# Threshold search on VectorE alone, rotations spread over four slabs

## The chip, the cores and the metric

The kernel runs on one core of one Trainium2 chip. The metric is the device time of one execution in microseconds (us), as a median of several runs. The core's engines are called as in the profile: PE (TensorE matmul) with PEld (its weight load), DVE (VectorE), ACT (ScalarE), POOL (GpSimd) and SP (SyncE, which here only issues DMAs). Each engine works through its own list of instructions in order; semaphores tie the lists together.

## What is computed

The program is two whole transformer blocks over 1024 tokens of width 1024. Only the second block's input projection and the selection of keys matter here:

```python
h = rms_norm(x, norm_mix[i])
proj = h @ w_in[i]
(r_q, r_k, r_v, r_g, d_q, d_c, d_pe, d_g,
 i_q, i_k, i_w) = jnp.split(proj, split_at, axis=-1)
r_q = rotary(r_q.reshape(B, S, RET_HEADS, RET_DK), positions, RET_THETA)
r_k = rotary(r_k.reshape(B, S, RET_HEADS, RET_DK), positions, RET_THETA)
...
q_pe = rotary(d_q[..., :DSA_ROPE], positions, ROPE_THETA)
...
score = jnp.einsum('bth,bths->bts', wi, rel).astype(jnp.float32)
score = jnp.where(valid[None], score, -jnp.inf)
top_val, top_idx = lax.top_k(score, n_sel)     # n_sel = 256
```

The kernel does not sort. For each query row it finds the value of the 256th largest score by fixing the 32 bits of a float one after the other: for each bit it counts how many scores lie at or above a candidate, and keeps the bit if there are at least 256.

## The kernel before

`build` runs ten stages one after the other; at the end of a stage's block all engines meet. The stage of this case is `stage_project`.

**TensorE** computes the projection in `product` (L1538 to L1542): a float32 product is three matmuls of 128x512 (high by high, high by low, low by high), here called a triple. The weights come in pieces of 128x512, one for each of eight k's of a slab of 512 columns. Slabs `R_Q` and `R_K` are made in four halves of four token tiles (`queries`); the score matmuls stand between those triples. `R_V`, `R_G`, `D_Q` and `D_G` follow in a loop over `slab(j)`, with all eight token tiles for each piece, so a piece of them is eight triples. A bank is filled again only when it has been evacuated (`ev`).

**A piece's way**: SP loads it (L2049) into one of four buffers, once PE has finished the piece four before it (`um`). ACT copies it to the rounded high part (`split`, L2142), POOL subtracts to get the low part (L2249), and PE waits for that (`lo`). So a piece can be ready three pieces ahead of PE.

**ACT** also evacuates the banks to `PJ` (`evacuate`, L2147), with Silu for the two gates. During the search its list is written by a planner: `begins` and `ends` foretell with `TRIPLE` = 0.68 us when PE will want a piece and when a bank is ready, `BIT` = 4.9 us is a bit of the search, and `slab_work` puts splits and evacuations between the bits accordingly.

**POOL** also rotates `R_Q` and `R_K`. A `turn` of one token tile is one `cmul` of six tensor_tensors (L374 to L379). In the passes n = 5 and 6 (the slabs `R_V` and `R_G`) one turn follows every piece's subtraction, sixteen in all. In the last pass four smaller ones rotate `D_Q`.

**DVE** makes the scores `NM` (L2295) and then searches. The score rows of the six token tiles with more than 256 keys have 384, 512, 640, 768, 896 and 1024 elements. In `count` DVE compares the two widest to 0 or 1 (L2305, uint8 into `junk`) and ACT sums them (L2228, `counted`); the four narrower ones DVE compares and sums in one instruction (L2308). Three instructions on 128x6 integers then follow: the comparison with 256 (L2311, after the wait for ACT), the keeping of the bit (`copy_predicated`, L2318), and the next candidate (L2316). After the stage comes `stage_retention`, whose first matmuls are at L2360.

Of the kernel before, what the change touches and what calls it, by code (L numbers as in the profile page):

```python
# [17 lines left out]
F32 = mybir.dt.float32  # L18
# [10 lines left out]
KT = D // P  # L29
# [1947 lines left out]
def stage_project(K):  # L1977
# [33 lines left out]
    cnt, need = columns(NB), columns(NB)  # L2011
    K.thr, K.cnt, K.need = thr, cnt, need
    w_in = [K.sem(f"pj_win{s}") for s in range(NR)]
    names = "prm hi lo um tm ev angr tab rope rms itr iev smm relr used cmp counted chain pchain".split()
    S = {n: K.sem("pj_" + n) for n in names}
    R_Q, R_K, R_V, R_G, D_Q, D_G = range(6)
    slabs = [None, R_Q, R_K, R_V, R_G, D_Q, D_G]
# [7 lines left out]
    for half in range(2):  # L2025
        quota[turned[half]] = (half + 1) * KT * NH
    ahead = [KT + q // NH + 2 for q in quota]
    TRIPLE, BIT = 0.68, 4.9

    def begins(u):  # L2030
        return TRIPLE * ((u - KT) * NH if u < 5 * KT else 4 * KT * NH + (u - 5 * KT) * NT) - TRIPLE * beside

    def ends(q):
        j, i = 2 + q // NT, q % NT
        return begins((3 + i // NH + 1) * KT if j == 2 else (j + 3) * KT) - TRIPLE * (NH - i % NH if j == 2 else NT - i)

    def table(t, lo, n, heads):
        return t[:, :, lo:lo + n].unsqueeze(2).to_broadcast([P, NT, heads, n])

    with nc.Block() as block:  # L2040
# [92 lines left out]
        @block.scalar  # L2133
        def _(act):
            arrived = [0] * NR

            def split(j, ks):
                cols = N_MIX if j == 0 else HALF
                for k in ks:
                    arrived[k % NR] += 32 if j == 0 else 16  # L2140
                    act.wait_ge(w_in[k % NR], arrived[k % NR])
                    nc.scalar.activation(part[k % NR][0][:, 0:cols], raw[k % NR][:, 0:cols], ACT.Copy).then_inc(S["hi"], 1)  # L2142

            def evacuate(j, i, bank):
                dst = K.MS[:, i, :] if j == 0 else K.PJ[:, slabs[j], i, :]
                func = ACT.Silu if slabs[j] in (R_G, D_G) else ACT.Copy
                nc.scalar.activation(dst, bank[:, 0:N_MIX if j == 0 else HALF], func).then_inc(S["ev"], 1)  # L2147

            def take_half(half):
                for i in range(NH):  # L2150
                    if i < NH - 1:
                        act.wait_ge(S["tm"], NT - 1 + half * (NH - 1) + i + 1)
                    else:
                        act.wait_ge(S["um"], (half + 2) * KT)
                    evacuate(1 + half // 2, half % 2 * NH + i, K.bank[i + (NH if half == 3 else 0)])

            def take_first():
                for i in range(NT):
                    if i < NT - 1:
                        act.wait_ge(S["tm"], i + 1)  # L2160
                    else:
                        act.wait_ge(S["um"], KT)
                    evacuate(0, i, K.bank[i])

            def take_one(q):
                j, i = 2 + q // NT, q % NT
                if j == 2:
                    half = 2 + i // NH
                    if i % NH < NH - 1:
                        act.wait_ge(S["tm"], NT - 1 + half * (NH - 1) + i % NH + 1)  # L2170
                    else:
                        act.wait_ge(S["um"], (half + 2) * KT)
                elif j == len(slabs) - 1:
                    act.wait_ge(S["um"], NP * KT)
                elif i < NT - 1:
                    act.wait_ge(S["tm"], NT - 1 + 4 * (NH - 1) + (j - 3) * (NT - 1) + i + 1)
                else:
                    act.wait_ge(S["um"], (j + 3) * KT)
                evacuate(j, i, K.bank[i])

            def slab_work(made, taken, until):
                while True:
                    more = made < NP * KT and begins(made) - 8.0 < until
                    done = taken < NT * (len(slabs) - 2) and ends(taken) - 1.5 < until
                    if not more and not done:
                        return made, taken
                    if more and (not done or begins(made) - 8.0 < ends(taken) - 1.5):
                        split(made // KT, range(made % KT, made % KT + 1))
                        made += 1
                    else:  # L2190
                        take_one(taken)
                        taken += 1

            split(0, range(4))
            act.wait_ge(S["angr"], 1)
            nc.scalar.activation(sin[:], red[:], ACT.Sin).then_inc(S["tab"], 1)
            nc.scalar.activation(cos[:], quar[:], ACT.Sin).then_inc(S["tab"], 1)
            split(0, range(4, KT))
            split(1, range(3))
            take_first()  # L2200
            split(1, range(3, lead // NH + 1))
            for i in range(NT):
                act.wait_ge(S["itr"], i + 1)
                b = K.bank[4 + i % 4]
                nc.scalar.activation(iqT[:, :, i * P:(i + 1) * P], b[:, 0:2 * P].rearrange("p (m t) -> p m t", m=2), ACT.Copy)
                nc.scalar.activation(ikT[:, i * P:(i + 1) * P], b[:, 2 * P:3 * P], ACT.Copy).then_inc(S["iev"], 1)
            act.wait_ge(S["rms"], 1)
            nc.scalar.activation(ss[:], ss[:], ACT.Sqrt).then_inc(S["rms"], 1)
            made = KT + lead // NH + 1
            for n in range(len(groups)):  # L2210
                for m in range(4 * n, 4 * n + 4):
                    i, h, c, e = pieces[m]
                    act.wait_ge(S["smm"], n + 1)
                    if m >= 4:
                        act.wait_ge(S["used"], m - 3)
                    nc.scalar.activation(rel[m % 4][:, 0:e - c], K.bank[4 + m % 4][:, 0:e - c], ACT.Relu, scale=IDIM ** -0.5).then_inc(S["relr"], 1)
                while made < ahead[n]:
                    split(made // KT, range(made % KT, made % KT + 1))
                    made += 1
                if n in turned:  # L2220
                    take_half(turned.index(n))
            act.wait_ge(S["used"], len(pieces))
            made, taken = slab_work(made, 0, 3.0)
            for b in range(32):
                for j in range(NB - 2, NB):
                    x = junk[:, packed(j + 2)]
                    act.wait_ge(S["cmp"], 2 * b + j - (NB - 2) + 1)
                    nc.scalar.activation(x, x, ACT.Copy, accum_out=cnt[:, j:j + 1]).then_inc(S["counted"], 1)  # L2228
                made, taken = slab_work(made, taken, 3.0 + BIT * (b + 1))
            slab_work(made, taken, 1.0e6)  # L2230

        @block.gpsimd
        def _(pool):
# [11 lines left out]
            for n in range(NP):  # L2245
                cols = N_MIX if n == 0 else HALF
                for k in range(KT):
                    pool.wait_ge(S["hi"], n * KT + k + 1)
                    g.tensor_tensor(part[k % NR][1][:, 0:cols], raw[k % NR][:, 0:cols], part[k % NR][0][:, 0:cols].bitcast(F32), ALU.subtract).then_inc(S["lo"], 1)  # L2249
                    if k == 0 and n == 1:  # L2250
                        pool.wait_ge(S["tab"], 2)
                    if n in (5, 6):
                        turn(n - 4, 0, FREQ_R, slice(k, k + 1))
                    elif n == NP - 1 and k >= 4:
                        turn(5, FREQ_R, FREQ_A, slice(2 * (k - 4), 2 * (k - 3)))

        @block.vector
        def _(dve):
# [41 lines left out]
            for i in range(NT):  # L2300
                link(v.memset(K.NM[0:RCHUNK, packed(i)][:, P * (i + 1) - RCHUNK:], LOW))

            def count(bound, b):
                for j in range(NB - 2, NB):
                    v.tensor_scalar(junk[:, packed(j + 2)], K.NM[:, packed(j + 2)], bound(j), None, ALU.is_ge).then_inc(S["cmp"], 1)  # L2305
                for j in range(NB - 2):
                    x = K.NM[:, packed(j + 2)]
                    last = v.tensor_scalar(junk[:, packed(j + 2)], x, bound(j), 0.0, ALU.is_ge, ALU.add, accum_out=cnt[:, j:j + 1])  # L2308
                link(last)
                dve.wait_ge(S["counted"], 2 * (b + 1))  # L2310
                link(v.tensor_scalar(keep[:], cnt[:], TOPK - 0.5, None, ALU.is_ge))  # L2311

            count(lambda j: 0.0, 0)
            link(v.tensor_scalar(thr[:], keep[:], 1, None, ALU.subtract))
            for bit in range(30, -1, -1):
                link(v.tensor_scalar(cand[:], thr[:], 1 << bit, None, ALU.bitwise_xor))  # L2316
                count(lambda j: cand[:, j:j + 1].bitcast(F32), 31 - bit)
                link(v.copy_predicated(thr[:], keep[:], cand[:]))  # L2318


def stage_retention(K):
# [708 lines left out]
```

## Time and profile before

| what | value |
|---|---|
| median of 3 runs | 2340.78 us (2338.63 to 2342.23) |
| the profiled execution, its own time | 2344.68 us |
| its span | 2342.9 us |
| PE busy | 2152.0 us, 92% |
| DVE busy | 1261.3 us, 54% |
| ACT busy | 783.0 us, 33% |
| POOL busy | 414.2 us, 18% |
| mean granted TensorE clock | 0.958 |

Times in the rows count from the span's start. A number in square brackets at the end of a row of the timeline is the engine's idle time just before the row, with what ended it. "PEclk" is the clock granted to TensorE as a share of the full 2.4 GHz. The stage in question ends at about 1856 us, and the search begins at 1613 us.

### The profile page before, as it was taken

Reading aid. Unit: us, or ns where it says so; the run is one execution under the profiler, and the core shown is the slowest. Engines: PE = TensorE matmul, PEld = TensorE weight load, DVE = VectorE, ACT = ScalarE, POOL = GpSimd, SP = SyncE. Lnnn points to the kernel's source line nnn. Section 1 sums busy time; section 2 is a strip of 40 time slices with the busy share of each in tenths; the row PEclk is TensorE's granted clock in tenths of the full one; section 3 lists DMA queues with packets and bytes.
Section 4 is the critical chain, followed back from the end, with each engine's and each line's share of the span. In section 5 each row is a group of like instructions: output and inputs, shape, how many; then the busy total and the mean of one; then the engine's idle time right before and its main releaser. Section 6 shows DMA issues by size and latency. Waiting matters only on the chain. (4 is left out here: it accounts for less than half of the span.)

```text
span 2342.9 us, 27640 instructions
## 1 busy us (share of the span) xinstructions
PE 2152.0 (92%) x10421; PEld 1578.9 (67%) x10421; DVE 1261.3 (54%) x2170; ACT 783.0 (33%) x1396; POOL 414.2 (18%) x485
## 2 busy tenths in 40 slices
PE   7998999996979999999999995989789877989998
PEld 3744564593448888888888884956567774758876
DVE  6581893395753333224553225289999077862433
ACT  2222111210013322223443224266446244761415
POOL 2900011040000000000000002224782450300110
PEclk9999999997979999999999997999999998989999
DMA  8533110003223332343343332212111102003201
GB/s 316 153 128 121 39 36 1 1 1 135 72 81 96 93 98 85 94 153 108 111 123 109 89 90 67 60 46 77 32 41 39 33 1 80 1 1 126 72 1 72
DMA packets 187510, 180.55 MB, mean 77 GB/s; under 512 B 12982, under 2 KB 157686, under 8 KB 184074
## 3 DMA queue, kind: packets, MB, share of 16 engines
q1 hardware_dynamic: 184426, 168.61, 23.1%
q0 software_dynamic: 2880, 10.49, 1.2%
q8 instruction: 67, 1.10, 0.2%
q14 instruction: 41, 0.34, 0.0%
q10 hardware_dynamic: 96, 0.02, 0.0%
HBM read 165.18 MB, written 12.60 MB: 76 GB/s over the span
## 5 line engine op out<-in xcount | busy, mean ns | idle before, releaser
L1729 DVE TENSOR_TENSOR ff_part<-ff_raw,ff_part 128x1024 fp32r<-128x1024 f32 (+2 forms) x152 | 164.9, 1085 | 434.7 <-ACT ff_part L1643 434.6
L1643 ACT ACTIVATE ff_part<-ff_raw 128x1024 fp32r<-128x1024 f32 (+2 forms) x152 | 144.0, 948 | 433.8 <-PE ps L1542 431.6
L1540 PE MATMUL ps<-h,ff_part 128*128 128x512 f32 x704 | 275.6, 391 | 4.4 <-DVE ff_part L1729 4.4
L1541 PE MATMUL ps<-h,ff_part 128*128 128x512 f32 x704 | 274.9, 390 | 0.0
L1542 PE MATMUL ps<-h,ff_part 128*128 128x512 f32 x704 | 274.9, 390 | 0.0
L1540 PE MATMUL ps<-pj_part,h 128*128 128x512 f32 (+1 forms) x448 | 182.2, 407 | 39.1 <-POOL pj_part L2249 28.1
L1541 PE MATMUL ps<-pj_part,h 128*128 128x512 f32 (+1 forms) x448 | 176.6, 394 | 0.0
L1542 PE MATMUL ps<-pj_part,h 128*128 128x512 f32 (+1 forms) x448 | 176.0, 393 | 0.0
L1540 PEld LDWEIGHTS ps<-h,ff_part 128*128 128x128 f32 x704 | 132.8, 189 | 32.2 <-DVE ff_part L1729 4.8
L1542 PEld LDWEIGHTS ps<-h,ff_part 128*128 128x128 f32 x704 | 132.7, 189 | 27.8
L1541 PEld LDWEIGHTS ps<-h,ff_part 128*128 128x128 f32 x704 | 132.9, 189 | 27.6
L1540 PEld LDWEIGHTS ps<-pj_part,h 128*128 128x128 f32 x448 | 86.4, 193 | 77.5 <-POOL pj_part L2249 34.7
L1540 PE MATMUL ps<-ff_hid,ff_part 128*128 128x512 f32 x352 | 136.9, 389 | 0.0
L1541 PE MATMUL ps<-ff_hid,ff_part 128*128 128x512 f32 x352 | 136.9, 389 | 0.0
L1542 PE MATMUL ps<-ff_hid,ff_part 128*128 128x512 f32 x352 | 136.9, 389 | 0.0
L2249 POOL TENSOR_TENSOR pj_part<-pj_raw,pj_part 128x512 fp32r<-128x512 f32 (+1 forms) x72 | 93.8, 1308 | 195.3 <-ACT pj_part L2142 195.2
L1540 PE MATMUL ps<-w_end,se_hT 128*128 128x512 f32 x256 | 106.9, 418 | 0.4 <-DVE se_hT L2959 0.4
L1000 PE MATMUL ps<-mx_w,HT 128*128 128x272 f32 (+1 forms) x320 | 106.2, 493 | 0.0
L1542 PE MATMUL ps<-w_end,se_hT 128*128 128x512 f32 x256 | 99.9, 390 | 0.0
L1541 PE MATMUL ps<-w_end,se_hT 128*128 128x512 f32 x256 | 99.7, 389 | 0.0
L1542 PEld LDWEIGHTS ps<-pj_part,h 128*128 128x128 f32 x448 | 86.5, 193 | 17.0
L2228 ACT ACTIVATE pj_junk<-pj_junk 128x896 uint8<-128x896 uint8 x64 | 64.0, 1002 | 98.6 <-DVE pj_junk L2305 96.9
(572 smaller groups left out, 4005.0 us busy)
## 6 DMA issues: line engine op xcount, KB each, us to landing
ff_raw<-in_w_ffn_in SPq DMA_DIRECT2D x88, 512.0 KB, 3.7
s_wm<-in_w_mod SPq DMA_DIRECT2D x16, 1024.0 KB, 4.9
pj_raw<-in_w_in SPq DMA_DIRECT2D x64, 256.0 KB, 2.6
ff_raw<-in_w_ffn_out SPq DMA_DIRECT2D x32, 384.0 KB, 3.3
ff_raw<-in_w_ffn_out SPq DMA_DIRECT2D x32, 320.0 KB, 3.1
mod_w<-in_w_mod SPq DMA_DIRECT2D x8, 1024.0 KB, 9.0
mod_x<-in_x SPq DMA_DIRECT2D x8, 512.0 KB, 14.5
w_out<-in_w_out SPq DMA_DIRECT2D x4, 1024.0 KB, 8.6
```

Of the source, the lines that this page charges most:

```text
L1000: mm = nc.tensor.matmul(bank[:, 0:cols], lhs, rhs, start=(k == 0), stop=(k == KT - 1))
L1540: nc.tensor.matmul(out, w[0], x[0], start=first, stop=False)
L1541: nc.tensor.matmul(out, w[0], x[1], start=False, stop=False)
L1542: return nc.tensor.matmul(out, w[1], x[0], start=False, stop=last)
L1643: nc.scalar.activation(part[s % 2][0][:, 0:n, :], raw[s][:, 0:n, :], ACT.Copy).then_inc(hi, 1)
L1729: v.tensor_tensor(part[s % 2][1][:, 0:n, :], raw[s][:, 0:n, :], part[s % 2][0][:, 0:n, :].bitcast(F32), ALU.subtract).then_inc(lo, 1)
L2228: nc.scalar.activation(x, x, ACT.Copy, accum_out=cnt[:, j:j + 1]).then_inc(S["counted"], 1)
L2249: g.tensor_tensor(part[k % NR][1][:, 0:cols], raw[k % NR][:, 0:cols], part[k % NR][0][:, 0:cols].bitcast(F32), ALU.subtract).then_inc(S["l ...
```

## The change

- `count`: DVE compares and sums all six tiles itself with the instruction of L2308. ACT's sums (L2228) and the semaphores `cmp` and `counted` go.
- The small steps are two for each bit instead of three: `keep` becomes the bit's weight where fewer than 256 scores were counted (is_lt, mult), and one `scalar_tensor_tensor` on integers takes that bit out of the candidate and puts the next one in. `copy_predicated` is gone.
- The planner (`begins`, `ends`, `take_one`, `slab_work`) is gone. ACT's list is plain: the splits of the next slab's first three pieces, the evacuation of this slab, then the other five splits.
- POOL's sixteen turns of `R_Q` and `R_K` come after every second piece (k = 1, 3, 5, 7) in the passes n = 5 to 8. The four of `D_Q` stay where they were, behind the turn if there is one.

```diff
-            def slab_work(made, taken, until):
...
+            for u in range(made, 4 * KT + 3):
+                split(u // KT, range(u % KT, u % KT + 1))
+            take_half(2)
+            split(4, range(3, KT))
+            split(5, range(3))
+            take_half(3)
+            split(5, range(3, KT))
+            for j in range(3, len(slabs)):
+                if j + 3 < NP:
+                    split(j + 3, range(3))
+                take(j)
+                if j + 3 < NP:
+                    split(j + 3, range(3, KT))
...
-                    if n in (5, 6):
-                        turn(n - 4, 0, FREQ_R, slice(k, k + 1))
-                    elif n == NP - 1 and k >= 4:
+                    if n >= 5 and k % 2:
+                        t = 4 * (n - 5) + k // 2
+                        turn(1 + t // NT, 0, FREQ_R, slice(t % NT, t % NT + 1))
+                    if n == NP - 1 and k >= 4:
                         turn(5, FREQ_R, FREQ_A, slice(2 * (k - 4), 2 * (k - 3)))
...
-            def count(bound, b):
-                for j in range(NB - 2, NB):
-                    v.tensor_scalar(junk[:, packed(j + 2)], K.NM[:, packed(j + 2)], bound(j), None, ALU.is_ge).then_inc(S["cmp"], 1)
-                for j in range(NB - 2):
+            def count(bound, weight):
+                for j in range(NB):
                     x = K.NM[:, packed(j + 2)]
                     last = v.tensor_scalar(junk[:, packed(j + 2)], x, bound(j), 0.0, ALU.is_ge, ALU.add, accum_out=cnt[:, j:j + 1])
                 link(last)
-                dve.wait_ge(S["counted"], 2 * (b + 1))
-                link(v.tensor_scalar(keep[:], cnt[:], TOPK - 0.5, None, ALU.is_ge))
-
-            count(lambda j: 0.0, 0)
-            link(v.tensor_scalar(thr[:], keep[:], 1, None, ALU.subtract))
+                link(v.tensor_scalar(keep[:], cnt[:], TOPK - 0.5, float(weight), ALU.is_lt, ALU.mult))
+
+            count(lambda j: 0.0, -1)
+            link(v.tensor_scalar(cand[:], keep[:], 1 << 30, None, ALU.bitwise_xor))
             for bit in range(30, -1, -1):
-                link(v.tensor_scalar(cand[:], thr[:], 1 << bit, None, ALU.bitwise_xor))
-                count(lambda j: cand[:, j:j + 1].bitcast(F32), 31 - bit)
-                link(v.copy_predicated(thr[:], keep[:], cand[:]))
+                count(lambda j: cand[:, j:j + 1].bitcast(F32), 1 << bit)
+                link(v.scalar_tensor_tensor(out=(cand if bit else thr)[:], in0=keep[:], scalar=(1 << bit) >> 1, in1=cand[:],
+                                            op0=ALU.bitwise_xor, op1=ALU.bitwise_xor))
```

## Rows read from the trace of the kernel before

**Rows 1.** The page: engine PE, and the loads of pieces (KB, us to landing).

```profile
PE   2152.0 (92%) x10421; PEld 1578.9 (67%) x10421; DVE 1261.3 (54%) x2170; ACT 783.0 (33%) x1396; POOL 414.2 (18%) x485
...
pj_raw<-in_w_in SPq DMA_DIRECT2D x64, 256.0 KB, 2.6
```

**Rows 2.** Waits of PE, 1613 to 1857 us: total, times, longest.

```profile
PE ps L1540 <- POOL pj_part L2249: 21.1, 15, 6.4
PE ps L1540 <- ACT PJ L2147: 10.9, 3, 6.9
```

**Rows 3.** Windows, L1540 alone (one matmul of each triple): length, PE busy (count).

```profile
1613.10:1852.20 239.10, 116.86 (x288) 55.10 (x288) 0.96 0.15 41
1780.00:1850.00 70.00, 39.95 (x103) 19.24 (x103) 1.00 0.14 38
```

**Rows 4.** Windows, all engines: PE, PEld, DVE, ACT, POOL busy (count), PEclk, DMA.

```profile
1757.40:1767.50 10.10, 5.93 (x14) 4.73 (x15) 9.60 (x27) 10.07 (x20) 1.76 (x2) 0.50 0.00 1
...
1619.90:1809.30 189.40, 157.39 (x650) 123.39 (x649) 184.90 (x395) 93.37 (x177) 116.65 (x126) 0.95 0.16 42
```

**Rows 5.** Timeline of PE: start, length, idle before in brackets.

```profile
1666.40 0.50 PE L1540 MATMUL ps<-pj_part,h 128*128 128x512 f32 x1 [1.21 <-POOL pj_part L2249]
...
1761.57 0.80 PE L1540 MATMUL ps<-pj_part,h 128*128 128x512 f32 x1 [6.89 <-ACT PJ L2147]
...
1856.53 2.79 PE L2360 MATMUL ps<-ident,PJ 128*128 128x128 f32 x12 [4.37 <-PEq L2040]
```

**Rows 6.** ACT, 1613 to 1857 us: its waits, a group, and its last work.

```profile
ACT pj_junk L2228 <- DVE pj_junk L2305: 96.9, 31, 5.2
...
L2142 ACT ACTIVATE pj_part<-pj_raw 128x512 fp32r<-128x512 f32 x38 | 23.3, 622 | 17.3 <-DMA pj_raw<-in_w_in 17.3
...
1852.20 4.03 ACT L2147 ACTIVATE PJ<-ps 128x512 f32<-128x512 f32 x8 [18.51 <-PE ps L1542]
```

**Rows 7.** Timeline of POOL in pass n = 5: subtraction, turn begins, next subtraction.

```profile
1672.02 1.26 POOL L2249 TENSOR_TENSOR pj_part<-pj_raw,pj_part 128x512 fp32r<-128x512 f32 x1 [0.56 <-ACT pj_part L2142]
1673.25 0.73 POOL L374 TENSOR_TENSOR pj_pscr<-PJ,prm 128x256 f32<-128x256 f32 x1
...
1678.97 1.26 POOL L2249 TENSOR_TENSOR pj_part<-pj_raw,pj_part 128x512 fp32r<-128x512 f32 x1 [0.55 <-ACT pj_part L2142]
```

**Rows 8.** Timeline of DVE: the search's beginning, and its last bit.

```profile
1613.13 3.33 DVE L2305 TENSOR_SCALAR pj_junk<-NM 128x896 uint8<-128x896 f32 x2
...
1807.92 0.17 DVE L2311 TENSOR_SCALAR prm<-prm 128x6 int32<-128x6 f32 x1
...
1808.54 1.35 DVE L2305 TENSOR_SCALAR pj_junk<-NM,prm 128x896 uint8<-128x896 f32 x2
1809.81 0.60 DVE L2308 TENSOR_SCALAR_CACHE_REDUCE pj_junk<-NM,prm 128x384 uint8<-128x384 f32 x1
...
1810.34 0.74 DVE L2308 TENSOR_SCALAR_CACHE_REDUCE pj_junk<-NM,prm 128x512 uint8<-128x512 f32 x1
...
1811.81 1.00 DVE L2308 TENSOR_SCALAR_CACHE_REDUCE pj_junk<-NM,prm 128x768 uint8<-128x768 f32 x1
...
1812.86 0.90 DVE L2311 TENSOR_SCALAR prm<-prm 128x6 int32<-128x6 f32 x1
```

**Rows 9.** DVE's small steps: groups (busy, mean ns), and one line's min/median/max ns.

```profile
L2318 DVE COPY_PREDICATED prm<-prm 128x6 int32<-128x6 int32 x31 | 15.7, 505 | 1.1
L2316 DVE TENSOR_SCALAR prm<-prm 128x6 int32<-128x6 int32 x31 | 13.7, 441 | 1.1
L2311 DVE TENSOR_SCALAR prm<-prm 128x6 int32<-128x6 f32 x32 | 11.7, 366 | 1.3 <-ACT pj_junk L2228 0.3
...
L2316 DVE TENSOR_SCALAR prm<-prm x31: 170/649/1247, 1620.3 to 1808.3; 128x6 int32<-128x6 int32 x31
```

**Rows 10.** Timeline: two-input steps of DVE, two without and two with POOL's subtraction.

```profile
1556.33 1.54 DVE L2295 SCALAR_TENSOR_TENSOR NM<-pj_rel,prm,NM 128x512 f32<-128x512 f32 x2
...
1557.12 2.44 DVE L2295 SCALAR_TENSOR_TENSOR NM<-pj_rel,prm,NM 128x512 f32<-128x512 f32 x2
...
1557.71 1.30 POOL L2249 TENSOR_TENSOR pj_part<-pj_raw,pj_part 128x512 fp32r<-128x512 f32 x1 [2.48 <-ACT pj_part L2142]
```

More of the change, by code:

```diff
@@ L2013, in stage_project @@
     w_in = [K.sem(f"pj_win{s}") for s in range(NR)]
-    names = "prm hi lo um tm ev angr tab rope rms itr iev smm relr used cmp counted chain pchain".split()
+    names = "prm hi lo um tm ev angr tab rope rms itr iev smm relr used chain pchain".split()
     S = {n: K.sem("pj_" + n) for n in names}
@@ L2027, in stage_project @@
     ahead = [KT + q // NH + 2 for q in quota]
[L2028 to L2035, printed above, removed]
     def table(t, lo, n, heads):
@@ L2163, in take_first, with take @@
                     evacuate(0, i, K.bank[i])
[L2165 to L2170, printed above, removed]
-                    else:
[L2172 to L2179, printed above, removed]
-            def slab_work(made, taken, until):
[L2182 to L2192, printed above, removed]
+            def take(j):
+                if j == len(slabs) - 1:
+                    act.wait_ge(S["um"], NP * KT)
+                for i in range(NT):
+                    if i < NT - 1:
+                        act.wait_ge(S["tm"], NT - 1 + 4 * (NH - 1) + (j - 3) * (NT - 1) + i + 1)
+                    else:
+                        act.wait_ge(S["um"], (j + 3) * KT)
+                    evacuate(j, i, K.bank[i])
             split(0, range(4))
@@ L2222, in _ @@
             act.wait_ge(S["used"], len(pieces))
-            made, taken = slab_work(made, 0, 3.0)
-            for b in range(32):
-                for j in range(NB - 2, NB):
[L2226 to L2230, printed above, removed]
+            for u in range(made, 4 * KT + 3):
[11 more added lines that the diff above has]
+                    split(j + 3, range(3, KT))
         @block.gpsimd
@@ L2301, in _ @@
                 link(v.memset(K.NM[0:RCHUNK, packed(i)][:, P * (i + 1) - RCHUNK:], LOW))
-            def count(bound, b):
-                for j in range(NB - 2, NB):
-                    v.tensor_scalar(junk[:, packed(j + 2)], K.NM[:, packed(j + 2)], bound(j), None, ALU.is_ge).then_inc(S["cmp"], 1)
-                for j in range(NB - 2):
+            def count(bound, weight):
+                for j in range(NB):
                     x = K.NM[:, packed(j + 2)]
```

## The prediction

> **What bounds the kernel now.** I read the page first: PE is busy for 2152.0 us of the span [rows 1], so what counts is where PE stands still or runs slowly in the stage that the change touches. The view of waits gives 21.1 us for POOL's low parts and 10.9 us for ACT's evacuations after the search has begun [rows 2]. The windows give the whole loss: PE works through 288 triples from 1613.1 to 1852.2 us, 239.1 us, whereas from 1780 to 1850 us, with no stall, 103 triples take 70.0 us, 0.680 us each [rows 3]. At that rate 288 triples take 195.8 us. So PE loses 43.3 us. 32.0 us of it are the two waits; some is restarting, as the first matmul after a stall takes 0.50 us; and the rest is the clock: from 1757.4 to 1767.5 us PEclk is 0.50 (1.2 GHz), around a stall of 6.89 us [rows 4, 5].
>
> The reader should see two causes. **POOL** in passes n = 5 and 6 does a subtraction and a turn for each piece, and its cycle is 6.95 us (1672.02 to 1678.97), whereas PE needs 8 x 0.680 = 5.44 us: PE waits 1.21 us for a typical piece [rows 5, 7]. **ACT** sat 96.9 us behind DVE's comparisons [rows 6]; a split or an evacuation listed behind such a wait comes when DVE's bit lets it, which is how the 6.9 us stall arises. The planner counts 4.9 us a bit, and DVE takes (1812.86 - 1613.13) / 32 = 6.24. After PE's last matmul, eight evacuations on ACT take 4.03 us and the next stage's first matmul comes at 1856.53 us [rows 5, 6]. DVE ended the search 40 us earlier and is not what bounds the stage [rows 8].
>
> **ACT's list.** The sums of L2228 go, and with them every wait for DVE. What is left for a slab is eight splits of 0.622 and eight evacuations, at 4.03 / 8 = 0.50 each [rows 6]: 9.0 us in 43.5, so ACT has time. Does the fixed order make PE wait? Ahead of an evacuation stand three splits. The third one's load is issued when the finishing slab has its last piece (5.44 us) to go, lands 2.6 us later [rows 1], and is split 0.6 us after that; the first evacuation can end some 1.7 us before PE wants its bank, and the others follow at 0.50 us where PE takes 0.68. The table load for the first Silu may cost some tenths once. The splits behind the evacuation are wanted only three pieces (16.3 us) later. I take nothing; if that cover fails, it is a rival below.
>
> **POOL's turns.** A turn takes 6.95 - 1.26 - 0.55 = about 5.15 us [rows 7]. Two pieces now cost POOL 2 x 1.26 + 5.15 = 7.7 us against PE's 10.9, where before they cost 13.9. The smaller `D_Q` turns are half as wide, so about 2.8 us each (estimate: half of 5.15, and a little for fixed costs). The heaviest stretch, k = 4 to 7 of the last pass, is 4 x 1.26 + 2 x 5.15 + 4 x 2.8 = 26.5 us against 21.8 of PE, but a low part can be made ahead: load 2.6, split 0.6 and subtraction 1.3 are 4.5 us of the 16.3 that three pieces last [rows 1, 6, 7], which leaves 11.8 us of cover for the backlog of 4.7. The longest thing in front of a subtraction is a turn with a `D_Q` turn behind it, 8 us, also under 11.8. So PE's wait for POOL goes wholly. SP's queue is not touched.
>
> **PE without stalls** ends at 1613.1 + 195.8 = 1808.9 us; the half clock goes with the stalls that preceded it. ACT's last evacuations make it 1813.0, and the next stage begins 0.3 us behind that, at 1813.3. By PE alone the gain is 1856.5 - 1813.3 = 43.2 us.
>
> **DVE.** A bit without POOL's interference costs now: three small steps 0.62 us (1807.92 to 1808.54), the two wide comparisons 1.27 (to 1809.81), and the four sums 2.93 with 0.11 to the next small step (to 1812.86) [rows 8]: 4.94 us. The new bit has six sums. Those of 384, 512 and 768 elements take 0.60, 0.74 and 1.00 us, and their starts go forward by 0.53 for the first and 0.93 to 0.94 for the widest [rows 8]: 0.133 us more for every 128 elements. Continued to 896 and 1024 that is 1.07 and 1.20, so 2.27 us in place of 1.27. The six come to 5.20, and with 0.11 and two small steps of 0.205 the quiet bit is 5.72 us.
>
> What POOL adds: a small step takes 0.17 us at least, but the means are 0.505, 0.441 and 0.366, with a median of 0.649 for L2316 [rows 9]; in the last bit L2311 took 0.90 beside a subtraction [rows 8]. The mean is 0.44, so 0.27 is added to a step while POOL is busy for 116.65 of 189.4 us, 62% [rows 4]. Afterwards POOL has, in the same stretch, some 40 subtractions of 1.27, 16 turns of 5.15 and four of 2.8: 144 us, 76%. That makes 0.27 x 76 / 62 = 0.33 for a step. Whether the new two-input integer step is delayed likewise no row shows. The nearest rows: two SCALAR_TENSOR_TENSORs of 512 take 1.54 us alone, and 2.44 when POOL subtracts beside them [rows 10], so I count it as delayed. The bit is then 5.31 + 2 x (0.205 + 0.33) = 6.38 us, 32 of them 204.2 us, and the search ends at 1613.1 + 204.2 = 1817.3 us, about 4 us behind ACT. For both sides: no delay gives 5.72 a bit and 1796.2 us (PE and ACT then end the stage); 0.66 us for every small step, as in most rows beside a turn, gives 5.31 + 2 x 0.69 = 6.69 and 1827.2 us.
>
> On this there is a rule. The Trainium skill (SBUF — State Buffer, section Who interferes with whom) says that DVE and GpSimd share one pair of ports as an exclusive lock, that a tensor_scalar contends when it can use two ports but not in the form that writes out its accumulator, and that a step with two SBUF inputs contends with a GpSimd instruction that reads SBUF. The trace agrees for the two kinds of tensor_scalar. By the rule the new counts would never be delayed and both small steps would, which is the sum that I take; read to exempt the integer step, it would be the 43 us case.
>
> **The sum.** The stage's end moves from 1856.5 to 1817.3 + 0.3 = 1817.6: 38.9 us less, after which the next stages run as they did. The profiled execution is 2344.68 us (its span and 1.8 us around it) and would be 2305.8; it lies 3.9 us above the median of 2340.78, so the median comes to 2301.9. The first pass compares with a constant and is a little quicker, so I say 2301.5.
>
> **Rivals.**
> - *PE stays the bound.* If the integer step is not delayed, a bit is 6.05 us, and DVE ends at 1806.7, before ACT at 1813.0. The gain is 43.2 us: 2297.6. For it: no row has this step. Against: rows 10.
> - *POOL delays every small step.* 1827.2 us, gain 29 us, 2311.8. For it: the turns now lie beside nearly all bits, and DVE's cycle could settle into step with POOL's. Against: POOL has 24% idle.
> - *The fixed ACT order stalls PE at slab ends.* Apart from the 6.9 us the waits for evacuations are 2.0 us each [rows 2]. At five boundaries, with 0.3 for restarting, 11.5 us: PE ends at 1820.4, ACT at 1824.5, 2309. Against: the 1.7 us of lead worked out above.
> - *Slower.* One mechanism: DVE, which had 40 us to spare, becomes the bound because each small step waits as long as the longest seen, 1.25 us [rows 9]. The bit is 5.31 + 2 x 1.28 = 7.87, and the end 1865.0: 9 us more, 2350. It decides from (1856.2 - 1613.1) / 32 = 7.60 us a bit. Against: that needs POOL to begin a long instruction just ahead of both steps in every bit.
>
> **Chances.** The forecast (DVE last, by up to some 8 us) 0.56; PE the bound 0.20; POOL delays all 0.13; stalls at slab ends 0.07; slower 0.03; a loss of nearly all the gain by something not named 0.01. The range reaches from just under the second case to the third, 2296 to 2312. About 0.2% is what a measurement of this kernel tells from no change. Faster 0.96, same 0.01, slower 0.03.
>
> **What would show it.** L2228 gone, and no wait of ACT for DVE; PE with about 103 triples in each 70 us from 1613 us to its end at 1809, PEclk 1.00 throughout; POOL's wait for ACT or loads ahead of most subtractions, and no PE wait for `pj_part`; DVE's sums of 896 and 1024 at 1.13 and 1.27 us; the period of a bit near 6.4 us; the SCALAR_TENSOR_TENSOR's mean near 0.5 and not 0.17 us. In the chain, the last thing before the next stage would be DVE's final small step at about 1817 us. Wrong would be: PE still waiting at slab ends, a bit over 6.7 us, or sums of the wide tiles that grow faster than 1.04 ns an element.

## The result, and the profile after

| | median, us | ratio to before, 95% interval |
|---|---|---|
| before | 2341.51 (4 runs) | |
| changed kernel | 2299.93 (4 runs) | 0.9821 (0.9806 to 0.9837) |
| forecast | 2301.5 (2296 to 2312) | |

The change saves 41.6 us, and the forecast misses the time by 1.6 us. But the stage does not end the way it was forecast. (Line numbers move from kernel to kernel: in the changed kernel L2284 is the sum of a tile, L2286 the comparison with 256, L2292 the new two-input step, L2138 the evacuation, L2226 the subtraction and L2335 the next stage's first matmul.) The view of waits for PE, from 1613 us on (total, times, longest), holds neither of the two waits of [rows 2] any more; the first that is left is the meeting at the stage's end:

```profile
PE ps L2335 <- PEq L2031: 4.4, 1, 4.4
```

The windows of all engines (length; PE, PEld, DVE, ACT, POOL busy; PEclk; DMA), from 1613.1 us to PE's last matmul of the stage, then from 1619 us to the search's end, stand against [rows 3, 4]:

```profile
1613.10:1808.20 195.10, 194.97 (x859) 160.77 (x857) 191.07 (x444) 39.50 (x70) 127.45 (x158) 1.00 0.19 50
1619.00:1807.40 188.40, 188.34 (x831) 155.62 (x830) 185.20 (x432) 36.97 (x64) 124.33 (x156) 1.00 0.18 49
```

PE needs 195.1 us where it needed 239.1, it is busy throughout, and its clock is 1.00 in the whole window. The ends of the three engines, from the timelines of ACT, DVE and PE:

```profile
1808.17 4.03 ACT L2138 ACTIVATE PJ<-ps 128x512 f32<-128x512 f32 x8 [18.46 <-PE ps L1542]
...
1801.38 0.17 DVE L2286 TENSOR_SCALAR prm<-prm 128x6 int32<-128x6 f32 x1
1801.58 0.17 DVE L2292 SCALAR_TENSOR_TENSOR prm<-prm 128x6 int32<-128x6 int32 x1
1801.78 0.61 DVE L2284 TENSOR_SCALAR_CACHE_REDUCE pj_junk<-NM,prm 128x384 uint8<-128x384 f32 x1
...
1807.10 0.17 DVE L2286 TENSOR_SCALAR prm<-prm 128x6 int32<-128x6 f32 x1
1807.31 0.17 DVE L2292 SCALAR_TENSOR_TENSOR prm<-prm 128x6 int32<-128x6 int32 x1
...
1812.50 2.79 PE L2335 MATMUL ps<-ident,PJ 128*128 128x128 f32 x12 [4.37 <-PEq L2031]
```

PE's last matmul ends at 1808.1, ACT's evacuations at 1812.2, and the next stage begins at 1812.50 us, against 1856.53 in [rows 5]. DVE ended its search at 1807.5, before both. So PE with ACT's tail is the bound, the first of the rivals. The search began at 1611.62 us here and at 1613.13 before [rows 8]; counted from there, the stage's end came 243.4 us later before and 200.9 now, 42.5 less.

DVE's groups (busy us, mean ns) show the two new sums and the small steps, and how much of the time is delay:

```profile
L2284 DVE TENSOR_SCALAR_CACHE_REDUCE pj_junk<-NM,prm 128x1024 uint8<-128x1024 f32 x31 | 39.5, 1275 | 0.0
L2284 DVE TENSOR_SCALAR_CACHE_REDUCE pj_junk<-NM,prm 128x896 uint8<-128x896 f32 x31 | 35.4, 1142 | 0.0
...
L2286 DVE TENSOR_SCALAR prm<-prm 128x6 int32<-128x6 f32 x32 | 12.5, 392 | 1.1
L2292 DVE SCALAR_TENSOR_TENSOR prm<-prm 128x6 int32<-128x6 int32 x31 | 10.9, 352 | 1.1
```

A quiet bit takes 1807.10 - 1801.38 = 5.72 us, exactly the sum of the prediction. The mean bit takes (1807.5 - 1611.6) / 32 = 6.12, where the prediction had 6.38: the small steps are delayed by 0.20 us each, not by 0.33.

### The profile page after: what moved, and what is told of

Its sections match the earlier page's. It is cut to its first block and busy times, and to the rows that moved or that the text cites. A ratio compares the mean times of both kernels' runs of the same rounds, so it can differ in the third digit from the quotient of the medians.

```text
span 2298.9 us, 27514 instructions
## 1 busy us (share of the span) xinstructions
PE 2140.2 (93%) x10421; PEld 1576.5 (69%) x10421; DVE 1257.4 (55%) x2203; ACT 717.9 (31%) x1268; POOL 402.5 (18%) x485
## 5 line engine op out<-in xcount | busy, mean ns | idle before, releaser
L1540 PE MATMUL ps<-h,ff_part 128*128 128x512 f32 x704 | 275.3, 391 | 4.5 <-DVE ff_part L1729 4.5
L1540 PE MATMUL ps<-pj_part,h 128*128 128x512 f32 (+1 forms) x448 | 178.0, 397 | 6.9 <-POOL pj_part L2226 6.7
L1541 PE MATMUL ps<-pj_part,h 128*128 128x512 f32 (+1 forms) x448 | 174.8, 390 | 0.0
L1542 PE MATMUL ps<-pj_part,h 128*128 128x512 f32 (+1 forms) x448 | 174.4, 389 | 0.0
L2284 DVE TENSOR_SCALAR_CACHE_REDUCE pj_junk<-NM,prm 128x384 uint8<-128x384 f32 (+1 forms) x186 | 163.7, 943 | 1.1
L1540 PEld LDWEIGHTS ps<-h,ff_part 128*128 128x128 f32 x704 | 132.7, 188 | 32.4 <-DVE ff_part L1729 4.9
L1540 PE MATMUL ps<-ff_hid,ff_part 128*128 128x512 f32 x352 | 136.9, 389 | 0.0
L2226 POOL TENSOR_TENSOR pj_part<-pj_raw,pj_part 128x512 fp32r<-128x512 f32 (+1 forms) x72 | 93.9, 1308 | 171.4 <-ACT pj_part L2133 170.1
L1540 PEld LDWEIGHTS ps<-pj_part,h 128*128 128x128 f32 x448 | 85.4, 191 | 37.4 <-issue 14.2
L1540 PE MATMUL ps<-w_end,se_hT 128*128 128x512 f32 x256 | 106.9, 418 | 0.4 <-DVE se_hT L2934 0.4
L2133 ACT ACTIVATE pj_part<-pj_raw 128x512 fp32r<-128x512 f32 (+1 forms) x72 | 45.4, 632 | 178.3 <-DMA pj_raw<-in_w_in 175.4
```

What stands on the lines that cost most here:

```text
L1540: nc.tensor.matmul(out, w[0], x[0], start=first, stop=False)
L1541: nc.tensor.matmul(out, w[0], x[1], start=False, stop=False)
L1542: return nc.tensor.matmul(out, w[1], x[0], start=False, stop=last)
```

## Experiments

The question was whether PE had waited for POOL's load, as the prediction has it, or for something else, and which of the change's parts did the work. Each kernel's time stands beside the kernel before of the same session, whose median lay between 2341.0 and 2342.5 us.

### The turns alone

```diff
 # before, and
-                    if n in (5, 6):
-                        turn(n - 4, 0, FREQ_R, slice(k, k + 1))
-                    elif n == NP - 1 and k >= 4:
+                    if n >= 5 and k % 2:
+                        t = 4 * (n - 5) + k // 2
+                        turn(1 + t // NT, 0, FREQ_R, slice(t % NT, t % NT + 1))
+                    if n == NP - 1 and k >= 4:
```

> Before with POOL's sixteen turns spread over four slabs, and nothing else. Theory A (coupling: in passes n = 5 and 6 of before a piece took 6.94 us because ACT's split came once per bit of DVE, and the bit was 6.94 us long): ACT still waits for DVE's comparisons once per bit, so PE goes on getting one piece per bit wherever a bit is over 5.44 us. With POOL less busy the bit falls to some 6.0 us; the gain is about half of the change's 42 us, 15 to 27 us: 2315 to 2327. Theory B (POOL's load alone, 6.4 of 6.94 us a piece, was what PE waited for): the 21.1 us of waits for POOL and the half clock behind them go, only the 10.9 us for ACT stay: gain 30 us or more, 2311 or less.

2333.68 us, ratio 0.9964 (0.9949 to 0.9979): a gain of 8.8 us, less than either theory gave. The waits of PE, with total, times and longest:

```profile
PE ps L1540 <- POOL pj_part L2249: 12.0, 12, 4.3
PE ps L1540 <- ACT PJ L2147: 12.0, 3, 6.6
```

POOL is now busy for 15.06 us of the stretch from 1650 to 1680 us, where it was for 27.09 before, and PE for 25.60 against 24.71: freeing POOL has hardly moved PE. DVE's wide comparisons come alternately quick and delayed:

```profile
1653.64 2.38 DVE L2306 TENSOR_SCALAR pj_junk<-NM,prm 128x896 uint8<-128x896 f32 x2
1659.62 1.35 DVE L2306 TENSOR_SCALAR pj_junk<-NM,prm 128x896 uint8<-128x896 f32 x2
1665.78 2.39 DVE L2306 TENSOR_SCALAR pj_junk<-NM,prm 128x896 uint8<-128x896 f32 x2
```

Two bits take 12.14 us (1653.64 to 1665.78), and ACT has one split in each. PE gets two pieces in 12.1 us, where it would need 10.9. That is the coupling of theory A. What theory A left out are three stalls of 4.3, 6.6 and 4.7 us (the kernel before has two such). At each of them ACT had gone through a bit of DVE's without the split or the evacuation that PE needed next: before the first one it has no split between 1669.25 and 1679.40 us.

### The planner's length of a bit alone

```diff
 # before, and
-    TRIPLE, BIT = 0.68, 4.9
+    TRIPLE, BIT = 0.68, 6.24
```

> Before with the planner's length of a bit set to 6.24 us, what it was in the trace, instead of 4.9. Theory A: more splits and evacuations are placed between two bits, so the stalls of 6.4 and 6.9 us, where a split stood one bit too late, go with their half clock, and part of the 1.4 us a piece: gain 10 to 30 us. Theory B: only the 6.4 and 6.9 us with their clock go, 10 to 17 us, and every piece of passes n = 5 and 6 still takes 6.94 us, since POOL is unchanged.

2316.68 us, ratio 0.9890 (0.9867 to 0.9913): 25.8 us from one number. Both theories had the two long stalls go, and they did; PE's two waits fell from 32.0 to 11.6 us. Besides, most pieces in passes n = 5 and 6 take 6.5 us and not 6.94. POOL's timeline shows why 6.5:

```profile
1676.09 1.28 POOL L2249 TENSOR_TENSOR pj_part<-pj_raw,pj_part 128x512 fp32r<-128x512 f32 x1
1677.32 0.74 POOL L374 TENSOR_TENSOR pj_pscr<-PJ,prm 128x256 f32<-128x256 f32 x1
...
1679.54 1.12 POOL L377 TENSOR_TENSOR PJ<-PJ,prm 128x256 f32<-128x256 f32 x1
1680.74 1.07 POOL L378 TENSOR_TENSOR PJ<-PJ,pj_pscr 128x256 f32<-128x256 f32 x1
1681.76 0.74 POOL L379 TENSOR_TENSOR PJ<-PJ,pj_pscr 128x256 f32<-128x256 f32 x1
1682.58 1.28 POOL L2249 TENSOR_TENSOR pj_part<-pj_raw,pj_part 128x512 fp32r<-128x512 f32 x1
```

Here POOL never waits: 1682.58 - 1676.09 = 6.49 us is its own load, with L377 and L378 at 1.12 and 1.07 us. In [rows 7] it waited 0.55 us for ACT in every cycle. So of the 6.94 us, 0.45 were the wait for DVE's bit, by way of ACT. The coupling also works the other way: with the longer bit the planner put the last sums between the last evacuations, DVE waited 8.95 us for ACT in its last bit, and PE stood still for 6.3 us at the stage's end, where it was 4.4 before:

```profile
1826.75 0.17 DVE L2311 TENSOR_SCALAR prm<-prm 128x6 int32<-128x6 f32 x1 [8.95 <-ACT pj_junk L2228]
```

### Both of these

```diff
 # before with the spread turns of the first experiment, and
-    TRIPLE, BIT = 0.68, 4.9
+    TRIPLE, BIT = 0.68, 6.0
```

> Before with both: POOL's turns spread over four slabs, and the planner's length of a bit set to 6.0 us (with the turns spread, a bit took 5.95 us on average; the planner's 4.9 left three stalls of 4.5 to 6.8 us there). ACT still sums two tiles and waits for DVE in every bit. Theory A (a list of ACT that foretells DVE's time wrongly, and a full POOL, are the causes; the division of the counting is none): PE loses only some tenths of a us where bits alternate between 4.9 and 7.2 us, and the gain is 33 to 41 us, 2301 to 2309. Theory C (as long as ACT waits for DVE in every bit, no fixed list fits bits of changing length): stalls of 1 to 2 us recur at every second piece, as in the run with the spread turns alone, and the gain stays at 20 to 30 us, 2312 to 2322.

2315.67 us, ratio 0.9883 (0.9867 to 0.9900): 26.5 us, inside theory C's range and, in the medians, no more than the planner's number brought alone. Its four runs spread from 2312.2 to 2320.4 us, wider than those of the other kernels, and the profiled one is the slowest of them. PE's waits:

```profile
PE ps L1540 <- POOL pj_part L2249: 7.3, 8, 3.0
PE ps L1540 <- ACT PJ L2147: 0.5, 1, 0.5
```

The stalls are fewer but return. As long as ACT stops in every bit for DVE, whose bits take 4.9 to 7.9 us here, this fixed list does not fit; that none would is likely, but no other was tried.

### The search alone

```diff
 # before, with the changed kernel's count and small steps, and
-            made, taken = slab_work(made, 0, 3.0)
-            for b in range(32):
...
-                made, taken = slab_work(made, taken, 3.0 + BIT * (b + 1))
-            slab_work(made, taken, 1.0e6)
+            slab_work(made, 0, 1.0e6)
```

> Before with the new search alone: DVE counts all six tiles in two small steps a bit, ACT does not count; ACT's list stays in the planner's order, POOL's turns stay in passes n = 5 and 6. Theory A: the whole gain is here, since the coupling of ACT to DVE was the cause: within 3 us of the changed kernel, 2298 to 2303. Theory B: POOL's stalls of 21 us and their clock stay: gain 10 to 20 us, 2321 to 2331.

2302.28 us, ratio 0.9826 (0.9804 to 0.9848): 40.2 us. Theory A holds, theory B falls: POOL's turns are where they were and the planner's order is kept, and no wait of PE for a piece is left in the view of waits. The edit takes ACT's waits for DVE away and leaves the order of its list, so the plain order of the changed kernel is not what brings the time. (Eight pieces still begin some 0.33 us late, too little for the view, as in the next kernel, which has the plain list and the same time within 0.3 us.)

### The changed kernel with the turns back in two slabs

```diff
 # the changed kernel, and
-                    if n >= 5 and k % 2:
-                        t = 4 * (n - 5) + k // 2
-                        turn(1 + t // NT, 0, FREQ_R, slice(t % NT, t % NT + 1))
-                    if n == NP - 1 and k >= 4:
+                    if n in (5, 6):
+                        turn(n - 4, 0, FREQ_R, slice(k, k + 1))
+                    elif n == NP - 1 and k >= 4:
```

> The changed kernel, but with POOL's turns where they were, one after each piece of passes n = 5 and 6. Theory A: freed of DVE, POOL's cycle is 1.29 + 4.5 = 5.8 us (a turn took 4.5 us in the changed kernel, 5.15 in before), 0.36 us over PE's 5.44; sixteen pieces lose 5.8 us against a cover of 11.8, so PE has no stall, and POOL's spreading brought nothing: within 3 us of the changed kernel, about 2300 (DVE's bits get longer beside 93 us of full POOL and may end the stage by 1 to 3 us). Theory B: a piece still costs POOL 6.4 us or more; sixteen lose 15.4, less the cover 11.8, and with a half clock: 4 to 12 us slower than the changed kernel, 2304 to 2312.

2302.05 us, ratio 0.9822 (0.9801 to 0.9844), within 3 us of the changed kernel. POOL's timeline, two subtractions and the turn between them:

```profile
1652.43 1.31 POOL L2226 TENSOR_TENSOR pj_part<-pj_raw,pj_part 128x512 fp32r<-128x512 f32 x1
...
1655.90 0.74 POOL L377 TENSOR_TENSOR PJ<-PJ,prm 128x256 f32<-128x256 f32 x1
1656.72 0.74 POOL L378 TENSOR_TENSOR PJ<-PJ,pj_pscr 128x256 f32<-128x256 f32 x1
1657.42 0.73 POOL L379 TENSOR_TENSOR PJ<-PJ,pj_pscr 128x256 f32<-128x256 f32 x1
1658.23 1.31 POOL L2226 TENSOR_TENSOR pj_part<-pj_raw,pj_part 128x512 fp32r<-128x512 f32 x1
```

The cycle is 5.80 us, of which the turn is 4.5: L377 and L378 take 0.74 us, since DVE's wide comparisons, beside which they took 1.1, are gone. Two points of the expectation did not come so. First, PE does lose something: the next stage's first matmul is at 1815.21 us, 203.5 us after the search's beginning (1611.68), where the changed kernel has 200.9. The loss lies in the second of the two passes, where every piece begins some 0.33 us late, as here between the matmuls at 1693.96 and 1694.39, which are otherwise 0.23 apart:

```profile
1693.96 0.39 PE L1542 MATMUL ps<-pj_part,h 128*128 128x512 f32 x1
1694.39 0.50 PE L1540 MATMUL ps<-pj_part,h 128*128 128x512 f32 x1
```

Eight times 0.33 are the 2.6 us. Sixteen pieces that are each 0.36 us too long make 5.8 us, and 2.6 of them came out: so the cover was 3.2 us, and not 11.8. Second, DVE did not get slower beside a full POOL but faster; its groups of small steps (busy us, mean ns), then rows of its timeline:

```profile
L2285 DVE TENSOR_SCALAR prm<-prm 128x6 int32<-128x6 f32 x32 | 8.1, 255 | 1.1
L2291 DVE SCALAR_TENSOR_TENSOR prm<-prm 128x6 int32<-128x6 int32 x31 | 5.3, 172 | 1.1
```

```profile
1652.15 0.23 DVE L2285 TENSOR_SCALAR prm<-prm 128x6 int32<-128x6 f32 x1
...
1657.94 0.24 DVE L2285 TENSOR_SCALAR prm<-prm 128x6 int32<-128x6 f32 x1
1658.21 0.17 DVE L2291 SCALAR_TENSOR_TENSOR prm<-prm 128x6 int32<-128x6 int32 x1
```

The search ended at 1797.5 us, 185.8 after its beginning. POOL's cycle and DVE's bit were both 5.8 us long, and the small steps fell into the same place of POOL's cycle each time: the first step ends at 1658.18 us as the turn's last instruction ends (1658.15), and the second is not delayed. All the bits between 1640 and 1722 us are like this, and those of the search alone, where the turns are as dense, too.

### Three small steps again

```diff
 # the changed kernel, and
-                link(v.tensor_scalar(keep[:], cnt[:], TOPK - 0.5, float(weight), ALU.is_lt, ALU.mult))
+                link(v.tensor_scalar(keep[:], cnt[:], TOPK - 0.5, None, ALU.is_ge))
...
-            link(v.tensor_scalar(cand[:], keep[:], 1 << 30, None, ALU.bitwise_xor))
...
+            link(v.tensor_scalar(thr[:], keep[:], 1, None, ALU.subtract))
             for bit in range(30, -1, -1):
-                count(lambda j: cand[:, j:j + 1].bitcast(F32), 1 << bit)
-                link(v.scalar_tensor_tensor(out=(cand if bit else thr)[:], in0=keep[:], scalar=(1 << bit) >> 1, in1=cand[:],
-                                            op0=ALU.bitwise_xor, op1=ALU.bitwise_xor))
+                link(v.tensor_scalar(cand[:], thr[:], 1 << bit, None, ALU.bitwise_xor))
+                count(lambda j: cand[:, j:j + 1].bitcast(F32), 31 - bit)
+                link(v.copy_predicated(thr[:], keep[:], cand[:]))
```

> The changed kernel with the three small steps of before in each bit (comparison, copy_predicated, next candidate) instead of two. DVE ended its search 4.7 us before ACT's last evacuation (1807.5 against 1812.2 us). If DVE stands right behind PE as that says, 31 more small steps of 0.2 us and their delay of 0.2 make DVE end 12 us later, at about 1820, and the stage and the time 7 to 9 us later than the changed kernel: about 2308. If a small step is delayed by 0.33 us, as the prediction had it, it is 12 us later. If DVE's search does not count for the stage's end, no change: 2300. The rows also show whether the two-input step was delayed less (0.19 us on average) because it is two-input: then the third step and the second are delayed by 0.3 us here.

2306.72 us, ratio 0.9848 (0.9832 to 0.9864): 6.8 us more than the changed kernel. PE's last matmul began at 1806.42 us, and then PE stood still, until DVE was through:

```profile
1816.84 0.17 DVE L2293 COPY_PREDICATED prm<-prm 128x6 int32<-128x6 int32 x1
...
1817.55 0.66 PE L2335 MATMUL ps<-ident,PJ 128*128 128x128 f32 x2 [10.74 <-PEq L2031]
```

Counted from the search's beginning, DVE needed 206.8 us here and 195.9 in the changed kernel. The third step cost 10.9 us in all, 0.35 a bit; 6.4 us of it came out at the stage's end, the rest was cover. So some 7 us of the whole gain hang on there being two small steps and not three. The steps' means are 342, 279 and 444 ns: delays of 0.17, 0.11 and 0.27, so the two-input step of the changed kernel (0.19) is not delayed less than others.

### Four bits less

```diff
 # the changed kernel, and
-            for bit in range(30, -1, -1):
+            for bit in range(30, 3, -1):
...
-                link(v.scalar_tensor_tensor(out=(cand if bit else thr)[:], in0=keep[:], scalar=(1 << bit) >> 1, in1=cand[:],
+                link(v.scalar_tensor_tensor(out=(cand if bit > 4 else thr)[:], in0=keep[:], scalar=(1 << bit) >> 1 if bit > 4 else 0, in1=cand[:],
```

> The changed kernel with the lowest four bits of the threshold left out (27 counts after the first instead of 31). DVE's search ends 24.5 us earlier. If PE and ACT's last evacuations end the stage, the time stays within 0.1% of the changed kernel: 2300. If DVE were last, as the forecast said, it would fall by the distance between DVE's end and ACT's, 4 us.

2299.96 us, ratio 0.9819 (0.9802 to 0.9835), as the changed kernel. DVE's last step was at 1783.57 us; ACT's tail came when it always comes:

```profile
1809.24 4.03 ACT L2138 ACTIVATE PJ<-ps 128x512 f32<-128x512 f32 x8 [18.50 <-PE ps L1542]
```

The search began at 1612.66 us in this trace and the next stage at 1813.58, 200.9 us later, as in the changed kernel. So DVE is off the path that sets the end; it does not set it at 6.12 us a bit; at 6.46, with three small steps, it did.

### No turns

```diff
 # the changed kernel, and
-                    if n >= 5 and k % 2:
-                        t = 4 * (n - 5) + k // 2
-                        turn(1 + t // NT, 0, FREQ_R, slice(t % NT, t % NT + 1))
```

> The changed kernel without POOL's sixteen turns of R_Q and R_K (that rotation is left out). POOL falls from 66% busy to about 30% during the search. If POOL's work is what delays DVE's small steps, their mean falls from 0.39 and 0.35 us to about 0.25, and a bit from 6.12 to about 5.9 us; quiet bits show 5.72. The time stays at the changed kernel's 2300, because PE is the bound; a fall of over 2 us would mean that POOL or DVE still cost PE something.

2300.60 us, ratio 0.9822 (0.9805 to 0.9838): the same time with half of POOL's work gone: it is busy for 56.0 us of the stretch from 1619 to 1800, 31%. The two-input step's mean is down to 241 ns, from 352, and the comparison's to 194, from 392:

```profile
L2289 DVE SCALAR_TENSOR_TENSOR prm<-prm 128x6 int32<-128x6 int32 x31 | 7.5, 241 | 1.1
L2283 DVE TENSOR_SCALAR prm<-prm 128x6 int32<-128x6 f32 x32 | 6.2, 194 | 1.1
```

### A shorter tail

ACT's eight evacuations behind the last matmul wait for all of PE, since slab `D_G` lies over the buffers of the pieces. Six of its tiles lie over the buffers of pieces k = 4 to 6 only.

```diff
 # the changed kernel, and
-                if j == len(slabs) - 1:
-                    act.wait_ge(S["um"], NP * KT)
+                final = j == len(slabs) - 1
+                if final:
+                    act.wait_ge(S["um"], NP * KT - 1)
                 for i in range(NT):
-                    if i < NT - 1:
+                    if i < NT - (2 if final else 1):
```

> The changed kernel once more, unchanged, for a comparison on the same chip with the next one: 2300 us.

> The changed kernel, but six of the eight evacuations of the last slab start as their banks are finished, once PE has done the last piece but one (whose buffers they overwrite), instead of after PE's very last matmul. If PE and ACT's tail end the stage, the tail of 4.0 us falls to two evacuations, 1.1 us, and the time by 2.9 us: about 2297. DVE, which ended 0.7 us before PE, must not become last; if it does by drawing level, the gain is a few tenths less. If the stage's end is set elsewhere: no change.

The changed kernel 2298.97 us, 0.9825 (0.9811 to 0.9838); with the shorter tail 2295.94 us, 0.9807 (0.9794 to 0.9821). The intervals of the two ratios overlap, but the runs do not (2298.7 to 2302.7 us against 2295.3 to 2297.3); the medians differ by 3.0 us as worked out, and ACT's timeline shows the tail of 1.08 us:

```profile
1801.55 3.94 ACT L2138 ACTIVATE PJ<-ps 128x512 f32<-128x512 f32 x6 [13.78 <-PE ps L1542]
1806.25 1.08 ACT L2138 ACTIVATE PJ<-ps 128x512 f32<-128x512 f32 x2 [0.76 <-PE ps L1542]
```

This is the fastest kernel of the study.

## Why the prediction was right, and where it was wrong

**PE's side held.** 288 triples at 0.680 us gave 195.8 us without stalls, and the window took 195.1. The loss of 43.3 us went, the half clock included. The gain by PE alone, 43.2 us, came as 42.5 from the search's beginning to the next stage, and 41.6 in the medians. ACT's fixed order cost next to nothing at the slab ends: the table load for the first Silu took 1.28 us and not some tenths, which used up the lead, and one piece began some 0.3 us late (at 1720.80 us). The quiet bit of 5.72 us was exact, and the sums of 896 and 1024 elements took 1142 and 1275 ns, on the line drawn through the narrower ones.

**The step that failed is DVE's delay.** It was scaled from the mean delay before, by POOL's busy share, to 0.33 us a step, on which DVE ended at 1817.3 us and was last. It was 0.20, and DVE needed 195.9 us instead of 204.2. Two things were mis-sized. POOL's share was 124.33 of 188.4 us, 66% and not 76%, mostly because a turn takes 4.5 us and not 5.15. With that share alone put right the delay would be 0.29 us and DVE would end at 1814.7 us, still last. The larger error is that the share does not set the delay: from 1634 to 1727 us POOL was busy for 88.26 of 93 us with the turns dense and for 61.63 in the changed kernel, and the two steps took 252 and 166 ns on average beside the fuller POOL, 431 and 361 beside the other; without the turns, at 31%, the two-input step still took 241. What counts is where in POOL's cycle a step falls.

That the time came within 1.6 us is in part luck. The forecast had the next stage begin 204.5 us after the search's beginning (1613.1 to 1817.6) and the rival "PE stays the bound" 200.2; it took 200.9. The range holds both cases, so the time alone does not tell them apart; the ends of the engines do. That rival had the right end but the wrong reason, since it let the integer step escape the delay. (In [rows 10] the two pairs share an instruction, so the 0.9 us fell on one step; that a two-input step is delayed stands.) It does not escape; in the changed kernel, the timelines of DVE and POOL:

```profile
1696.05 0.65 DVE L2286 TENSOR_SCALAR prm<-prm 128x6 int32<-128x6 f32 x1
1696.73 0.66 DVE L2292 SCALAR_TENSOR_TENSOR prm<-prm 128x6 int32<-128x6 int32 x1
...
1695.93 0.73 POOL L378 TENSOR_TENSOR PJ<-PJ,pj_pscr 128x256 f32<-128x256 f32 x1
1696.62 0.74 POOL L379 TENSOR_TENSOR PJ<-PJ,pj_pscr 128x256 f32<-128x256 f32 x1
```

Each of the two steps ends as a POOL instruction ends. Here the rule of the Trainium skill (SBUF — State Buffer, section Who interferes with whom), that a step with two SBUF inputs contends with a GpSimd instruction that reads SBUF, agrees with the trace, at 0.66 us for a step of 0.17. So does its rule that the accumulating form does not: the sums of 1024 elements took 1275 ns on average with and without the turns.

**The attribution was half right.** The prediction saw the wait for POOL and called POOL's load the cause. But POOL's wait of 0.55 us for ACT in [rows 7] has DVE behind it. ACT's timeline in the kernel before, ahead of the two subtractions of [rows 7]:

```profile
1669.06 0.95 ACT L2228 ACTIVATE pj_junk<-pj_junk 128x896 uint8<-128x896 uint8 x1 [4.12 <-DVE pj_junk L2305]
...
1671.26 0.62 ACT L2142 ACTIVATE pj_part<-pj_raw 128x512 fp32r<-128x512 f32 x1
1676.01 0.95 ACT L2228 ACTIVATE pj_junk<-pj_junk 128x896 uint8<-128x896 uint8 x1 [4.13 <-DVE pj_junk L2305]
...
1678.21 0.61 ACT L2142 ACTIVATE pj_part<-pj_raw 128x512 fp32r<-128x512 f32 x1
```

There is one split for each bit of DVE, and the bit is 6.95 us long, as POOL's cycle is. The runs take a piece of passes n = 5 and 6 apart:

| a piece took | us | what went |
|---|---|---|
| before | 6.94 | |
| planner's bit 6.24 | 6.49 | 0.45: one split per bit of DVE |
| search on DVE alone, turns dense | 5.80 | 0.69: turns lengthened beside DVE's comparisons |
| turns spread | 5.44 | 0.36: POOL's own load |

Beside the new search only the last line is left for POOL's spreading to cure, and with the cover it is worth 2.6 us in the trace. The search on DVE alone brought 40.2 of the 41.6 us: it took ACT out of DVE's rhythm and DVE's wide comparisons out of POOL's way. Spreading the turns alone brought 8.8, the planner's number alone 25.8, both 26.5. The gains don't add, as they remove in part the same stalls. The traces show it more finely, if one counts from the beginning of the search to the next stage's first matmul. That distance is 200.8 or 200.9 us in all four traces in which nothing was changed for PE (the changed kernel twice, four bits less, no turns):

| kernel | us |
|---|---|
| before | 243.4 |
| turns alone | 235.9 |
| planner's length of a bit alone | 219.6 |
| both of these | 214.1 |
| search alone | 203.5 |
| changed, turns back in two slabs | 203.5 |
| changed, three small steps | 207.3 |
| changed | 200.9 |
| changed, shorter tail | 198.0 |

Here the turns bring 5.5 us on top of the planner's number, which the medians of those two kernels, known to 4 or 5 us, do not show.

**The cover of 11.8 us** for POOL's backlog was also too large where the turns begin: before pass n = 5 the pieces are half as long, so three pieces ahead are 3 x 2.72 = 8.2 us and not 16.3, less 4.5 for load, split and subtraction: some 3.7, near the 3.2 that the dense turns used. With the turns spread it did not matter; with the turns dense it showed.

**The slower rival** needed 7.60 us a bit for a loss, and a bit took 6.12. But DVE is close to being the bound again: at (1812.2 - 1611.6) / 32 = 6.27 us a bit it draws level with ACT's tail, only 0.15 us above what it takes, and with the third small step, at 6.46, it was last.

## What to carry to other kernels

When an engine waits for another by turns, the wait's name in the profile is only the last link: follow that engine's idle time too. Here POOL's 0.55 us for ACT, and ACT's 96.9 us for DVE, pointed to a rhythm that went when ACT no longer waited for DVE, even though DVE's own work for a bit grew from 4.94 to 5.72 us. Where a list is worked out from foretold times, look at those times first: putting 6.24 us, as measured, in place of the planner's 4.9 brought 26 us.

## What the runs showed of the hardware

- A GpSimd tensor_tensor of 128x256 takes 0.74 us, but 1.1 beside DVE's non-accumulating comparisons of 896 and 1024 elements (1.12 and 1.07 for L377 and L378 in two kernels with these, 0.74 for both in two kernels without). The delay goes both ways: DVE's pair took 1.35 us quiet and 2.39 beside the turns.
- DVE and POOL can fall into step. With both cycles at 5.8 us, in two kernels with dense turns, a POOL that was 95% busy (1634 to 1727 us) delayed the small steps less than one that was 66% busy with a changing distance: means of 252 and 166 ns in one of them and 282 and 166 in the other, against 431 and 361 in the same stretch.
